# S5 and the memory's split moved up by a block, and the SSD normalisation factor taken out of the output product

## What is computed

```
h = rmsnorm(x, mix_norm_w)
proj = h @ w_in                              # u 256 | z 768 | xbc 1792 | dt 12 columns
y_s5  = s5_mixer(u, ...)                     # state space scan, then y = gelu(y); y * sigmoid(y @ w_glu)
y_ssd = ssd_mixer(z, xbc, dt, ...)           # 12 heads; ends with
          y = y_diag + y_off + x * d_skip
          rmsnorm(y * silu(z), norm_w)       # over the 768 features of a token
x = x + concatenate([y_s5, y_ssd]) @ w_out
h = rmsnorm(x, xa_norm_w)
mem_n = rmsnorm(mem, mem_norm_w)             # 256 memory tokens
x = x + cross_attention(h, mem_n, wq, wk, wv, wo)
```

## Time and profile before

| | us |
|---|---|
| three runs: median (lowest to highest) | 1516.71 (1514.33 to 1518.45) |
| the profiled execution, device time | 1514.13 |
| its span | 1513.0 |
| TensorE busy | 1413.0 (93%) |
| VectorE busy | 980.3 (65%) |
| ScalarE busy | 752.8 (50%) |
| GpSimd busy | 142.3 (9%) |

### The profile page before, as it was taken

One profiled execution on the slowest core, in us unless ns is written; L12 is line 12 of the kernel. 1 busy time (PEld: TensorE's weight loads), 2 busy tenths in 40 slices (PEclk: granted clock), 3 DMA queues, 4 the chain that ended last, 5 costly groups with the idle time before them and its releaser, 6 DMA issues.

```text
span 1513.0 us, 18285 instructions
## 1 busy us (share of the span) xinstructions
PE 1413.0 (93%) x7292; PEld 1158.0 (77%) x7292; DVE 980.3 (65%) x1321; ACT 752.8 (50%) x966; POOL 142.3 (9%) x165
## 2 busy tenths in 40 slices
PE   7999989899999999999999998999998899999981
PEld 5788879687677888888887797887566788888861
DVE  4957666653355564455646468738545898899876
ACT  5764445444344322223234452345465788878863
POOL 1600012000000000000000312200000111111012
PEclk9999999999999999999999999999999899999996
DMA  6312314031123432332223221111015899999975
GB/s 212 113 69 98 127 58 138 29 111 56 56 66 119 164 101 77 130 100 95 75 78 113 84 84 56 56 56 57 0 48 208 320 409 424 406 425 414 402 292 194
DMA packets 39332, 231.62 MB, mean 153 GB/s; under 512 B 4400, under 2 KB 5696, under 8 KB 17104
## 3 DMA queue, kind: packets, MB, share of 16 engines
q1 hardware_dynamic: 30640, 200.09, 35.3%
q0 software_dynamic: 7648, 27.87, 4.9%
q10 hardware_dynamic: 960, 2.49, 0.4%
HBM read 213.66 MB, written 16.78 MB: 152 GB/s over the span
## 4 chain that ended last, share of the span: by engine, by line
PE 68%; DVE 8%; ACT 4%; issue 4%; DMA 1%; POOL 0%; POOLq 0%; DVEq 0%; ACTq 0%
PE bank L474 13%; PE bank L476 13%; PE bank L475 13%; PE bank L3182 5%; PE bank L3184 5%; PE bank L3183 5%; PE bank L620 2%; DVE w_lo L401 2%; PE bank L493 1%; PE bank L494 1%; PE bank L495 1%; PE bank L2411 1%; PE bank L2432 1%; ACT w_hi L395 1%; PE bank L2177 1%
## 5 line engine op out<-in xcount | busy, mean ns | idle before, releaser
L474 PE MATMUL bank<-h_hi,w_hi 128*128 128x512 f32 x952 | 380.9, 400 | 8.1 <-DVE w_lo L401 5.2
L476 PE MATMUL bank<-h_hi,w_lo 128*128 128x512 f32 x952 | 371.4, 390 | 0.0
L475 PE MATMUL bank<-h_lo,w_hi 128*128 128x512 f32 x952 | 371.2, 390 | 0.0
L401 DVE TENSOR_TENSOR w_lo<-w_raw,w_hi 128x2048 fp32r<-128x2048 f32 (+2 forms) x86 | 189.0, 2198 | 87.3 <-ACT w_hi L395 86.7
L474 PEld LDWEIGHTS bank<-h_hi,w_hi 128*128 128x128 f32 x952 | 179.1, 188 | 52.4 <-DVE w_lo L401 7.5
L476 PEld LDWEIGHTS bank<-h_hi,w_lo 128*128 128x128 f32 x952 | 179.0, 188 | 38.4
L475 PEld LDWEIGHTS bank<-h_lo,w_hi 128*128 128x128 f32 x952 | 179.2, 188 | 37.1 <-issue 2.2
L395 ACT ACTIVATE w_hi<-w_raw 128x2048 fp32r<-128x2048 f32 (+2 forms) x87 | 154.8, 1779 | 62.9 <-PE bank L476 62.9
L3367 DVE TENSOR_TENSOR h_lo<-w_raw,h_hi 128x2048 fp32r<-128x2048 f32 x32 | 73.2, 2291 | 10.5 <-ACT h_hi L3268 8.7
L3367 DVE TENSOR_TENSOR lo_b<-raw_b,hi_b 128x2048 fp32r<-128x2048 f32 x32 | 73.1, 2287 | 7.0 <-ACT hi_b L3268 6.9
L1813 ACT ACTIVATE gc<-gc 128x512 f32<-128x512 f32 x22 | 13.9, 632 | 111.4 <-DVE gc L1053 111.4
(11 more groups left out here) (610 smaller groups left out, 2744.8 us busy)
## 6 DMA issues: line engine op xcount, KB each, us to landing
w_raw<-in_params_dram SPq DMA_DIRECT2D x122, 1024.0 KB, 5.1
raw_b<-in_params_dram SPq DMA_DIRECT2D x51, 1024.0 KB, 8.3
w_raw<-in_params_dram SPq DMA_DIRECT2D x16, 704.0 KB, 4.0
result_rows<-osb POOLq DMA_DIRECT2D x16, 512.0 KB, 8.1
result_rows<-prm POOLq DMA_DIRECT2D x8, 512.0 KB, 3.2
xt<-in_x_t_dram POOLq DMA_DIRECT2D x1, 2048.0 KB, 9.1
scratch_rows<-htm SPq DMA_DIRECT2D x4, 512.0 KB, 2.9
out_dram<-pr SPq DMA_DIRECT2D x4, 512.0 KB, 2.6
```

The costliest lines, as they stand in the source:

```text
L401: V.tensor_tensor(k.w_lo[g % SPLIT][:, 0:size], k.raw[:, g % RAW, 0:size], k.w_hi[g % SPLIT][:, 0:size].bitcast(F32), ALU.subtract).then_i ...
L474: PE.matmul(ps, wh, hi[:, c, 0:width], start=c == 0, stop=False)
L475: PE.matmul(ps, wh, lo[:, c, 0:width], start=False, stop=False)
L476: m = PE.matmul(ps, wl, hi[:, c, 0:width], start=False, stop=c == parts - 1)
```

## The change

Input projection and S5:
- `pe_s5_in(0)` comes directly after the lag tables (which move to banks 6 and 7), without a wait for their copies; the memory's sum comes after x4; `pe_s5_out(0)` and `pe_s5_in(1)` after z1, `pe_s5_out(1)` after x5; the SSD sums and both halves of the gate product after z2.
- VectorE does the first rotation after its SSD steps, the second after z1, multiplies the memory by its norm after z2 (`dve_norm_mul`), then the gate. The memory's `m_hi` and `m_lo` come when the projection's last block has been copied to `pad`, ahead of that block's taps.
- ScalarE's gelu comes at z2, its sigmoid at x6, the memory's root after x4.
- Keys 0 and 1 are made together, part by part.

Output product:
- The SSD parts are split without the factor `rs` (`act_ssd_hi`, `dve_ssd_lo`: gain only), from head 9 on. Their products go to banks of their own (4 to 6), and the evacuation of an output block becomes three operations: bank times `rs`, xt plus S5's bank, plus the scaled one.
- S5's part of blocks 0 to 3 is done in steps 10 to 13 of the heads' loop. The filler turns are gone. The sum of squares goes to bank 7, after four parts of blocks 0 and 1.

```diff
@@ dve_residual
-    V.tensor_tensor(k.xt[:, blk, :], k.xt[:, blk, :], k.bank[i % 4][:, :], ALU.add).then_inc(s.evac_v, 1)
+    if stage == "w_out":
+        scaled = k.xdt[:, blk % 2, 0:T]
+        V.wait_ge(s.n_rs, NORM["ssd"] + 1)
+        k.v(V.tensor_tensor(scaled, k.bank[4 + blk % 3][:, :], k.rs[:, :], ALU.mult))
+        k.v(V.tensor_tensor(k.xt[:, blk, :], k.xt[:, blk, :], k.bank[i % 4][:, :], ALU.add))
+        k.v.own()
+        V.tensor_tensor(k.xt[:, blk, :], k.xt[:, blk, :], scaled, ALU.add).then_inc(s.evac_v, 1)
+    else:
+        V.tensor_tensor(k.xt[:, blk, :], k.xt[:, blk, :], k.bank[i % 4][:, :], ALU.add).then_inc(s.evac_v, 1)
@@ pe_w_in
             elif (part, n) == ("z", 0):
                 PE.wait_ge(s.s5_bt, 4)
                 pe_s5_lags(k)
+                pe_s5_in(k, 0)
+            elif (part, n) == ("x", 4):
+                PE.wait_ge(s.s5_bt, 4 + 2 * STEPS)
                 pe_norm_sum_all(k, "mem", k.msq, MEM, 7)
-            elif (part, n) == ("x", 4):
-                pe_s5_in(k, 0)
+            elif (part, n) == ("z", 1):
+                pe_s5_out(k, 0)
+                pe_s5_in(k, 1)
             elif (part, n) == ("x", 5):
-                pe_s5_in(k, 1)
-                pe_s5_out(k, 0)
-            elif (part, n) == ("x", 6):
                 pe_s5_out(k, 1)
-    for b in range(2):
-        pe_key(k, b)
-    pe_ssd_sums(k)
-    pe_s5_glu(k, 0)
+            elif (part, n) == ("z", 2):
+                pe_ssd_sums(k)
+                pe_s5_glu(k, 0)
+                pe_s5_glu(k, 1)
+    for c in range(DB):
+        for b in range(2):
+            pe_fm(k, "wk", 0, b, k.mhi, k.mlo, "mem", width=MEM, first=c, stop=c + 1)
     for b in range(2, EARLY_KEYS):
         pe_key(k, b)
-    pe_s5_glu(k, 1)
@@ act_w_in
+                    if blk == XBC_B - 1:
+                        for b in range(DB):
+                            act_norm_hi(k, "mem", k.msq, k.mhi, 0, b, MEM)
-            if q == 4:
-                A.wait_ge(s.gemm, BLOCK0["wk"])
-                for b in range(DB):
-                    act_norm_hi(k, "mem", k.msq, k.mhi, 0, b, MEM)
@@ dve_w_in
         if q == 1:
             dve_ssd_steps(k)
-        elif q in (2, 3):
-            dve_s5_step(k, q - 2)
-        if q in (3, 4):
-            dve_s5_skip(k, q - 3)
+            dve_split_to(k, SLOT0["zb"])
+            dve_s5_step(k, 0)
+        elif q == 2:
+            dve_split_to(k, SLOT0["zc"])
+            dve_s5_step(k, 1)
+            dve_s5_skip(k, 0)
+        elif q == 3:
+            dve_s5_skip(k, 1)
+            dve_norm_mul(k, "mem", k.mt, k.col("mem_norm", 0, DB), k.msq, k.rm, DB, MEM)
+            dve_s5_gate(k)
@@ pe_ssd, in the loop over steps
+        if step >= SSD_H - 2:
+            pe_out_s5(k, step - SSD_H + 2)
@@ new
+def ssd_part(blk):
+    return blk + 4 if blk < 4 else blk - 2
+
+def pe_out_ssd(k, b, first, stop):
+    PE, s = k.nc.tensor, k.s
+    g = SLOT0["w_out"] + b // 2
+    if first == 0:
+        if b < 2:
+            PE.wait_ge(s.sd_exp, 2 * SSD_H - 1 + b)
+        elif b == 2:
+            PE.wait_ge(s.sd_z, 5)
+        else:
+            PE.wait_ge(s.evac_v, EMPTIED[BLOCK0["w_out"] + b - 3][1])
+    ps = k.bank[4 + b % 3][:, :]
+    for blk in range(first, stop):
+        if b < 3:
+            PE.wait_ge(s.n_lo, N_HI["ssd"] + blk + 1)
...
+def dve_ssd_lo(k, blk):
+    V, s, x = k.nc.vector, k.s, ssd_part(blk)
+    V.wait_ge(s.n_hi, N_HI["ssd"] + blk + 1)
+    V.scalar_tensor_tensor(k.lo[:, x, :], k.sz[:, blk, :], k.col("ssd_norm", blk), k.hi[:, x, :].bitcast(F32), ALU.mult, ALU.subtract).then_inc(s.n_lo, 1)
@@ act_ssd, in and after the loop over heads
+        if h >= 9:
+            act_ssd_hi(k, h - 9)
+    act_ssd_hi(k, 3)
     ssd_square(k, 4)
+    act_ssd_hi(k, 4)
     ssd_square(k, 5)
-    act_norm_root(k, "ssd", k.rs[:, :], k.bank[4][:, :], SSD_W)
-    for b in range(6):
-        act_norm_hi(k, "ssd", k.xbc, k.hi, 2, b, T)
+    act_ssd_hi(k, 5)
+    act_norm_root(k, "ssd", k.rs[:, :], k.bank[7][:, :], SSD_W)
@@ dve_ssd, in and after the loop over heads
+        if h >= 10:
+            dve_ssd_lo(k, h - 10)
+    for b in range(2, 4):
+        dve_ssd_lo(k, b)
     dve_add_square(k, "ssd", k.xbc, 3, T)
     dve_ssd_gate(k, 5)
-    for b in range(4, 6):
-        dve_add_square(k, "ssd", k.xbc, b, T)
-    dve_norm_split(k, "ssd", k.sz, k.col("ssd_norm", 0, 6), k.xbc, k.rs, k.hi, k.lo, 2, 6, T)
+    dve_add_square(k, "ssd", k.xbc, 4, T)
+    dve_ssd_lo(k, 4)
+    dve_add_square(k, "ssd", k.xbc, 5, T)
+    dve_ssd_lo(k, 5)
@@ pe_memory
-    PE.wait_ge(s.o_lo, OUT["s5"] + 2)
-    for b in range(4):
-        pe_fm(k, "w_out", b // 2, b % 2, k.hi, k.lo, stop=2)
-        if b == 1:
-            pe_norm_sum(k, "ssd", k.xbc, T, 4)
-    pe_keep_on(k, 5, 8)
-    for b in range(DB):
-        pe_fm(k, "w_out", b // 2, b % 2, k.hi, k.lo, "ssd" if b < 4 else None, first=2 if b < 4 else 0, off=2)
+    pe_out_ssd(k, 0, 0, 4)
+    pe_out_ssd(k, 1, 0, 4)
+    pe_norm_sum(k, "ssd", k.xbc, T, 7)
+    pe_out_ssd(k, 0, 4, 6)
+    pe_out_ssd(k, 1, 4, 6)
+    for b in range(2, DB):
+        if b > 3:
+            pe_out_s5(k, b)
+        pe_out_ssd(k, b, 0, 6)
```

More of the change, by code:

```diff
@@ L127 @@
 N_ADD = counted(ssd=5, xa=7, ffn=7)
-N_MUL = counted(mix=DB, ssd=6)
+N_MUL = counted(mix=DB)
 N_HI = counted(mix=DB, ssd=6, xa=DB, ffn=DB)
@@ L554, in dve_norm_lo, with dve_norm_mul @@
     V.tensor_tensor(lo[:, off + b, 0:width], sq[:, b, 0:width], hi[:, off + b, 0:width].bitcast(F32), ALU.subtract).then_inc(s.lo, 1)
+def dve_norm_mul(k, name, src, gain, sq, rs, blocks, width):
+    V, s = k.nc.vector, k.norm(name)
+    V.wait_ge(s.rs, NORM.get(name, 0) + 1)
+    for b in range(blocks):
+        V.scalar_tensor_tensor(sq[:, b, 0:width], src[:, b, 0:width], gain[:, b:b + 1], rs[:, 0:width], ALU.mult, ALU.mult).then_inc(s.mul, 1)
 def dve_norm_split(k, name, src, gain, sq, rs, hi, lo, off, blocks, width, slot=None):
@@ L862, in act_s5_lags @@
         A.wait_ge(s.s5_turn, 5 + h)
-        lags = k.bank[5 + h][0:LANES, :].rearrange("p (t c) -> p t c", c=P)
+        lags = k.bank[6 + h][0:LANES, :].rearrange("p (t c) -> p t c", c=P)
         for e in range(STEPS):
@@ L885, in pe_s5_lags @@
             for part in range(2):
-                m = PE.matmul(k.bank[5 + h][0:LANES, t * P:t * P + P].rearrange("p (e c) -> p e c", e=STEPS), k.bd[:, part, n, 0, :],
+                m = PE.matmul(k.bank[6 + h][0:LANES, t * P:t * P + P].rearrange("p (e c) -> p e c", e=STEPS), k.bd[:, part, n, 0, :],
                               k.cb[:, part, 0:STEPS, n, :], start=part == 0, stop=part == 1)
@@ L1014, in act_s5_glu, with act_s5_hi @@
         A.activation(k.tmp[:, j, :], k.bank[4 + j][:, :], ACT.Sigmoid).then_inc(s.s5_sig, 1)
+def act_s5_hi(k):
+    A, s = k.nc.scalar, k.s
     for j in range(2):
@@ L1153, in act_w_in @@
             act_split_to(k, SLOT0[stage] + slot + 1)
+            if (part, n) == ("z", 2):
+                act_s5_gelu(k, 0)
+                act_s5_gelu(k, 1)
+            elif (part, n) == ("x", 6):
+                act_s5_glu(k)
             for j in range(2):
@@ L1194, in act_w_in @@
                 act_s5_bt(k)
+            elif (part, n) == ("x", 4):
+                act_norm_root(k, "mem", k.rm, k.bank[7][:, 0:MEM], D)
         if q == 1:
             act_s5_lags(k)
-            act_norm_root(k, "mem", k.rm, k.bank[7][:, 0:MEM], D)
             act_ssd_steps(k)
@@ L1222, in dve_w_in @@
                     blk = 2 * n + j
+                    if blk == XBC_B - 1:
+                        for b in range(DB):
+                            dve_norm_lo(k, "mem", k.msq, k.mhi, k.mlo, 0, b, MEM)
+                        dve_split_to(k, SLOT0["wk"] + 1)
                     V.wait_ge(s.tap0, blk + 1)
                     dve_taps(k, k.pad[:, blk % 2, :], 4, k.col("ssd_cw", 4 * blk, 4), k.xbc[:, blk, :], s.conv)
-            if part == "x" and n == 6:
-                dve_norm_split(k, "mem", k.mt, k.col("mem_norm", 0, DB), k.msq, k.rm, k.mhi, k.mlo, 0, DB, MEM)
-                dve_split_to(k, SLOT0["wk"] + 1)
             if (part, n) == ("x", 0):
@@ L1285, in pe_key @@
 def pe_key(k, b):
-    pe_fm(k, "wk", b // 2, b % 2, k.mhi, k.mlo, "mem" if b == 0 else None, width=MEM)
+    pe_fm(k, "wk", b // 2, b % 2, k.mhi, k.mlo, width=MEM)
 def pe_value(k, b):
@@ L1426, in act_ssd @@
     dt, da, acs, e1, u, d = ssd_small(k)
-    act_s5_gelu(k, 0)
     for b in range(EARLY_KEYS):
         act_key(k, b)
-    act_s5_gelu(k, 1)
-    act_s5_glu(k)
+        if b == 1:
+            act_s5_hi(k)
     A.wait_ge(s.sd_dve, 6)
@@ L1486, in dve_ssd @@
     V.tensor_copy(u, al).then_inc(s.sd_dve, 1)
-    dve_s5_gate(k)
     V.wait_ge(s.sd_pe, 2)
```

32 lines of the change are left out of this document (29 added, 3 removed).

## The result

| us | before | after |
|---|---|---|
| median of four runs each (lowest to highest) | 1517.06 (1514.33 to 1518.45) | 1501.97 (1499.58 to 1505.07) |
| the profiled execution, device time | 1514.13 | 1503.37 |
| its span | 1513.0 | 1502.2 |

The two medians of the table stand 15.1 us apart. Forecast were 1502.9 and 13.8 us less. The change is faster by 0.86%.

A forecast was written before the change was run, and what follows sets the result against it. TensorE, busy 1413.0 of 1513.0 us, was taken as the bound, losing time to waits and low clock. Part A's 3.4 plus part B's 10.4 made 13.8 us off the 1516.71 median: 1502.9 us, range 1498 to 1511.

The forecast's parts named there:

- Part A: Projection to first keys: S5 and the memory's split moved up recover 5.5 us less 1.7 and 0.4, gaining 3.4 us.
- The new gap: After the last projection product: TensorE waits 1.6 to 1.7 us for a bank copy, one `m_hi`, one `m_lo` and hand-overs.
- Key 2: After keys 0 and 1: TensorE waits 0.4 us for VectorE to make the next weight block's `lo`.
- Keys 0 and 1: First keys after the projection: their 48 products take 5.8 us, where before they took 9.3.
- The second rotation: S5 on VectorE: runs 137.6 to 146.6 us, wanted at 148.5; slack of 1.9 us, the smallest in part A.
- Part B: Heads' loop and output product without the norm factor: ends at 315.6 us instead of 326.0, gaining 10.4 us.
- The table load: ScalarE's root: load costs 1.28 us as traced; the skill's extra drain of about 1.38 us would delay `rs` 1.4 to 2.8.
- Rival 1: Both places: the stall moves to VectorE's queue, gain 7 to 10 us, about 1508; chance 0.24 together with rival 4.
- Rival 2: Later stages, such as the experts' weight loading: the gain is given back, 1515 us, within 4 of before; chance 0.10.
- Rival 4: Keys after the new gap: the clock falls, costing up to 5.8 us, 1508; chance 0.24 together with rival 1.
- Rival 3: Output product, 285 to 316 us: VectorE's three-operation evacuation sets the pace, deciding above 5.5 us a block; 1521 us; chance 0.06.
- The check of the last block: End of the output product: last `lo` comes 3.7 us after the last product, wanted after 4.8; failure costs at most 1.3.

The follow-up runs named there:

- cover: Changed kernel with the SSD decay sums moved from before the last projection slot to behind it; 1498.96 us, ratio 0.9896 to the kernel before.
- b_only: Kernel before with only the edits of the heads' loop, output product and `dve_residual`; 1503.84 us, ratio 0.9931.
- late_s5: Changed kernel with S5's products of output blocks 0 to 3 behind the last pair; 1508.46 us, ratio 0.9959 to the kernel before.
- extra3: Changed kernel with three more 128x512 VectorE multiplications in each output block's evacuation; 1516.24 us, ratio 1.0006 to the kernel before.
- s5_early: Kernel before with only S5's part of output blocks 0 to 3 moved into steps 10 to 13, norm factor kept; 1515.46 us, ratio 1.0004.
- a_only: Kernel before with only the edits of the projection, S5, memory and keys; 1508.96 us, ratio 0.9964.
- after_again: Changed kernel run again unchanged, as a yardstick; 1501.65 us, ratio 0.9908 to the kernel before.
- extra1: Changed kernel with one more 128x512 VectorE multiplication in each output block's evacuation; 1503.13 us, ratio 0.9921 to the kernel before.
- cover2: Changed kernel with the SSD sums behind the last projection slot and the decay columns' turning between keys 2 and 3; 1496.96 us, ratio 0.9881.

## Why the prediction was right

**Part A** was forecast at 3.4 us and brought 3.06. The new gap: 1.6 to 1.7 forecast, 1.60 in the row. Key 2: 0.4 forecast, 0.44. Keys 0 and 1: 5.8 forecast, 5.8. The second rotation: 137.6 to 146.6 forecast for the start of its first and last step, 138.07 and 147.00 in the trace; the output that needs it started at 148.88 without a wait (148.5 forecast). What is off is the size of the loss before, 5.5 us, by 0.4 at most; 0.2 of that lay ahead of part A, for after was 0.2 us late at 43.8 us already. `cover` shows the gap's 1.6 us by taking them away.

**Part B** was forecast at 10.4 us and brought 10.2 (10.4 in `b_only`'s median). Less the 3.0 us that part A moves all of it up, the forecast had the pair's end at 273.5 (273.7 measured), the last SSD `lo` between 279.3 and 280.5 (279.45), the root at 282.7 (282.96) and the query product at 312.6 (312.81). The covered `lm` wait is what `late_s5` puts back, 3.25 us. The wait for head 11 is 0.23, smaller than the 0.65 forecast. One sum of the prediction is off: 21 operations of VectorE that start 0.61 to 0.66 us apart from 268.46 on end at about 281.4 to 282.4, not at 282.3 to 283.5. They end at 279.45, which is 282.5 on the scale of before, because some depend on the one before and start up to 0.78 us behind it: 0.67 on average.

**The table load.** The rows of after:

```profile
280.33 0.69 ACT L540 ACTIVATE rs<-bank,eps 128x512 f32<-128x512 f32 x1 [0.83 <-PE bank L524]
281.03 1.28 ACT L542 ACT_TABLE_LOAD   x1
282.33 0.63 ACT L542 ACTIVATE rs<-rs 128x512 f32<-128x512 f32 x1
```

The load starts 0.01 us after the end of the ACTIVATE before it, and the instruction behind it starts 1.30 us after the load does, so the root costs what the earlier trace rows gave. The drain of about 1.38 us that the Trainium skill (ScalarE: Activation LUTs, What ACT_TABLE_LOAD costs) adds is not seen here.

**Rival 1** (VectorE's queue, 1508) did not come: the two places have no more wait than forecast. **Rival 2** (given back later) neither: 12.7 of 13.3 us are still there at 1157 us, and the ratio keeps 13.0. **Rival 4** (the clock falls after the new gap) did not come where it was named: 1.00 in 180 to 185 us, in after and in each run that has part A. (Its price, 0.12 x 48, also counts only half of the 96 products that it names.) But after was the lucky execution of the six that have the gap: the other five show a low stretch in 205 to 215 us, some 25 us behind it, at a price of 0.3 to 1.4 us (last section). The prediction had taken the low clock out of part A for good.

**Rival 3** did not come either, but the step that put it far off was wrong. The prediction had VectorE's pace at 4.8 us a block and the point from which it decides at TensorE's 5.5, and the kernel slower than before only from 7.8. The runs show other numbers for both. VectorE can't start before it has both the first SSD bank and the root:

```profile
281.28 0.39 PE L1498 MATMUL bank<-h_hi,w_lo 128*128 128x512 f32 x1
```

This is the last product of block 0, full at 281.67; the root ends at 282.96, and VectorE starts at 283.09. So it waited for the root, though its row names the bank. The profile infers who ended a wait from the events near its end, and block 1 was full at 283.05. The root has left TensorE's path but not VectorE's. By then TensorE has S5's part of blocks 0 to 3 and the SSD part of blocks 0 and 1 behind it, and it needs part 6 of the query's input at 316.89. So VectorE must do its eight blocks, three weight splits among them, in 33.8 us: 4.2 us a block, not 5.5. It did them in 32.6 us (283.09 to the end of the `lo` at 314.94 + 0.75), of which it sat idle for 2.55: 30.0 us of work, 3.8 a block. The spare is 3.8 us over the whole stage.

The work was less than 8 x 4.8 = 38.4 for two reasons. The larger: the stretch up to that `lo` holds 24 operations of evacuation, seven `lo`, five sums of squares and three splits, where eight times the block of the prediction has eight, eight and four; by the prediction's own prices that is 32.9 us. The smaller, 2.8 us: operations that don't depend on each other start 0.61 us apart (283.09 to 283.70) and not 0.69. At 4.8 a block VectorE would have been 4.6 us late. Two errors, a deadline too generous and a cost too high, cancelled, and that is luck. The check of the last block held: its `lo` ends 3.7 us after the last product's end (316.63 against 312.97), and it is asked for 4.8 us after the first query product starts (317.57 against 312.81).

The rule with the measured numbers gives a wait of 8 x 0.72 - 3.8 = 2.0 us for one more operation (1.62 measured as idle, 2.2 lost in the stage) and 24 x 0.72 - 3.8 = 13.5 for three (13.4 measured). At 5.9 us of work a block, the three more operations of `extra3`, the gain is zero. The expectation of `extra3` had the same rule on record before its run, with a spare of 4.3 us (2.6 idle and 1.7 of slack) and 13.0 as the result; working the spare out from the deadline came after.

## What to carry over

A factor common to all parts of a product can be taken out of it and applied to the result; its gain is the chain (sum, root, multiplication, split) that leaves the product's path, and it is whole only together with work to put in front of the parts that are late. Here the factor alone brought 4.5 of 10.2 us (`late_s5`) and the move alone nothing (`s5_early`). Cost the new evacuation by its deadline: from the moment when the first result and the factor are there to the moment when its last product is asked for, all blocks in between, weight splits included, and not by the pace of one block against one block. A gap that a move opens can often be closed with small work that lies nearby and waits for nothing, here 1.8 us at the query by moving one call.

## What the hardware showed beyond this

The clock does not follow from the waits alone. Behind the wait of 3.2 us for `lm` before the last pair (it ends at 273.38 in before, 271.42 in `a_only`, 271.46 in `late_s5`) the granted clock was 0.94 and 0.72 in 270 to 280 us of before, 1.00 in all of it in `a_only`, and 0.66 in 270 to 275 us of `late_s5`. And the changed kernel itself had it both ways behind the wait of 1.93 us near 208 us. The first row is of after, the second of `after_again`; the eight products of the group take 1.54 and 2.83 us:

```profile
208.40 1.54 PE L1412 MATMUL bank<-lm,btm 128*128 128x192 f32 x8 [1.93 <-DVE lm L1611]
```

```profile
208.38 2.83 PE L1412 MATMUL bank<-lm,btm 128*128 128x192 f32 x8 [1.93 <-DVE lm L1611]
```

The stretches of `after_again` around it:

```profile
205.00:210.00 5.00, 3.07 (x19) 2.87 (x18) 2.21 (x5) 2.94 (x3) 0.00 (x0) 0.85 0.02 5
210.00:215.00 5.00, 4.50 (x29) 4.30 (x28) 4.28 (x5) 0.39 (x1) 0.00 (x0) 0.81 0.00 0
```

At the query it was 12.0 us earlier than before where after was 13.3; the difference is the price of that stretch. After is the exception. Six executions have the gap of 1.6 us before the keys (after, `after_again`, `a_only`, `late_s5`, `extra1`, `extra3`), and the other five were granted 0.84 to 0.93 in 205 to 210 us and 0.73 to 0.82 in 210 to 215. The two that cover the gap (`cover`, `cover2`) and the three without part A (before, `b_only`, `s5_early`) were granted 1.00 there, with the same wait of 1.93 us; the last three have their low stretch in 180 to 185 us instead (0.77, 0.66 and 0.66). So part A as a rule moves a low stretch more than it removes one. Its gain stands even so: the row of head 10 starts at 263.0 us on average in the six and at 266.0 in the three. Whether the gap brings the later low stretch about is not shown; two executions without it are few, and the rest of the stretch is the same.

So one profile can mislead about a low stretch by some 1.3 us, and of the 3.9 us that 12 products took in before (2.7 at full clock) the change may claim only a part. While the clock was low the products of 128x512 started 0.43 us apart, against 0.228: the lower of the two levels, 1.2 GHz against 2.4.

Stages that no edit touches took up to 2.2 and 3.7 us more in one execution than in another (157.3 to 159.5 from `hq` to `hS`, 329.9 to 333.6 for the last), most of it by one or two low stretches more or less, at about 1.5 us each. Read the granted clock there before calling it scatter. A gain of 3 us can be read in the trace at the place where it arises; the end of one profile doesn't show it.
